# A two-layer pooling and latent-attention trunk on one Trainium2 core: earlier split of the latent key weights, down product's banks handed over one by one, a taller meta matrix

## What is computed

```python
for i in range(DEPTH):                      # DEPTH = 2
    # layer 0: trailing means over windows 2, 4, 8, 16, then a 256x256 product per group
    # layer 1: latent attention: c_q = rms(h @ w_dq), kv = h @ w_dkv (320 wide), 8 heads
    hp = layer_norm(ALPHA * hp + mix_p, ln_g[i, 0], ln_b[i, 0])
    hp = layer_norm(ALPHA * hp + swiglu(hp, ffn_w_gate[i], ffn_w_up[i], ffn_w_down[i]), ln_g[i, 1], ln_b[i, 1])

def swiglu(h, w_gate, w_up, w_down):        # 1024 -> 2816 -> 1024
    return (jax.nn.silu(h @ w_gate) * (h @ w_up)) @ w_down
```

## Time and profile before

| what | value |
|---|---|
| median of 3 runs | 2686.84 us (2685.57 to 2687.7) |
| the profiled execution | 2684.7 us, its span 2682.9 us |
| mean granted TensorE clock | 0.974 |
| TensorE matmuls busy | 2553.1 us (95%), 13203 matmuls |
| VectorE busy | 1005.3 us (37%) |
| ScalarE busy | 567.6 us (21%) |
| GpSimd busy | 585.6 us (22%) |
| DMA | 117.37 MB, 44 GB/s on average |
| both FFNs' gate and up matmuls | 6336, by the three lines 557 to 559 |

### The profile page before, as it was taken

The page is one execution under the profiler, slowest core; times in us unless marked ns, Lnnn a source line. Parts: engine busy times, 40 slices in busy tenths (PEclk is TensorE's granted clock), DMA queues, the critical chain, the costliest instruction groups (busy, mean ns, idle before and its releaser), DMA issues.

```text
span 2682.9 us, 34788 instructions
## 1 busy us (share of the span) xinstructions
PE 2553.1 (95%) x13203; PEld 2122.1 (79%) x13203; DVE 1005.3 (37%) x1489; ACT 567.6 (21%) x948; POOL 585.6 (22%) x290
## 2 busy tenths in 40 slices
PE   8899999999999889899999999988999999999996
PEld 7789888898889776585857584447889988899885
DVE  3433333333333642333333333422333333333336
ACT  2411011110111342332323232433111111111112
POOL 2422222222222410000000000232222222222225
PEclk9999999999999989999999999988999999999998
DMA  5201110111101111000000002232101111011111
GB/s 165 55 24 47 47 47 23 47 47 47 47 23 47 44 48 43 16 1 31 0 19 12 16 0 75 80 122 55 46 25 47 47 47 40 30 47 47 47 31 67
DMA packets 130114, 117.37 MB, mean 44 GB/s; under 512 B 8704, under 2 KB 117208, under 8 KB 130048
## 3 DMA queue, kind: packets, MB, share of 16 engines
q1 hardware_dynamic: 130064, 116.70, 14.6%
HBM read 110.81 MB, written 6.42 MB: 44 GB/s over the span
## 4 chain that ended last, share of the span: by engine, by line
PE 92%; DVE 4%; issue 2%; ACT 1%; POOL 0%; DMA 0%; SPq 0%; ACTq 0%; DVEq 0%
PE ps L557 22%; PE ps L558 21%; PE ps L559 21%; PE ps L922 4%; PE ps L911 4%; PE ps L806 2%; PE ps L895 2%; PE ps L978 1%; PE ps L780 1%; PE ps L822 1%; PE ps L811 1%; PE ps L627 1%; PE ps L953 1%; PE ps L851 1%; PE ps L937 1%
## 5 line engine op out<-in xcount | busy, mean ns | idle before, releaser
L557 PE MATMUL ps<-XH,WGH 128*128 128x368 f32 x2112 | 699.8, 331 | 17.6 <-POOL WGL L1700 13.5
L558 PE MATMUL ps<-XL,WGH 128*128 128x368 f32 x2112 | 700.0, 331 | 0.0
L559 PE MATMUL ps<-XH,WGL 128*128 128x368 f32 x2112 | 697.2, 330 | 0.0
L1452 DVE TENSOR_TENSOR XR<-XR,ps 128x1024 f32<-128x1024 f32 x378 | 461.5, 1221 | 105.7 <-PE ps L559 105.7
L557 PEld LDWEIGHTS ps<-XH,WGH 128*128 128x128 f32 x2112 | 398.5, 189 | 22.3 <-issue 18.9
L1437 DVE TENSOR_TENSOR HF<-SG,ps 128x368 f32<-128x368 f32 x132 | 71.0, 538 | 917.8 <-PE ps L559 912.6
L558 PEld LDWEIGHTS ps<-XL,WGH 128*128 128x128 f32 x2112 | 398.0, 188 | 1.8
L559 PEld LDWEIGHTS ps<-XH,WGL 128*128 128x128 f32 x2112 | 398.2, 189 | 0.0
L557 PE MATMUL ps<-WDH,HH 128*128 128x512 f32 (+1 forms) x792 | 329.4, 416 | 9.6 <-DVE XR L1452 9.6
L1691 POOL TENSOR_TENSOR HL<-HF,HH 128x368 fp32r<-128x368 f32 x132 | 129.8, 983 | 853.0 <-DVE HH L1441 853.0
L559 PE MATMUL ps<-WDH,HL 128*128 128x512 f32 (+1 forms) x792 | 314.9, 398 | 0.0
(11 more groups left out here) (205 smaller groups left out, 2725.8 us busy)
## 6 DMA issues: line engine op xcount, KB each, us to landing
RAWG<-ffn_w_gate SPq DMA_DIRECT2D x44, 512.0 KB, 4.7
RAWG<-ffn_w_up SPq DMA_DIRECT2D x44, 512.0 KB, 5.9
RAWD<-ffn_w_down SPq DMA_DIRECT2D x44, 512.0 KB, 3.7
CR<-cache_mla_l SPq DMA_DIRECT2D x64, 160.0 KB, 2.6
XR<-x_prompt SPq DMA_DIRECT2D x8, 512.0 KB, 12.4
WOP<-mla_w_o SPq DMA_DIRECT2D x4, 1024.0 KB, 5.0
WOA<-mla_w_o SPq DMA_DIRECT2D x1, 4096.0 KB, 17.3
o_y_prompt<-XR SPq DMA_DIRECT2D x8, 512.0 KB, 2.6
```

The costliest lines, as they stand in the source:

```text
L557: pe.matmul(out, w[0], x[0], start=start, stop=False)
L558: pe.matmul(out, w[0], x[1], start=False, stop=False)
L559: return pe.matmul(out, w[1], x[0], start=False, stop=stop)
L1452: dve.tensor_tensor(XR[0:r, t, :], XR[0:r, t, :], bank2(4 + 2 * w, r), ALU.add).then_inc(s_row[2 * l + 1], 1)
```

## The change

There are three parts, and line numbers of the new kernel are about 10 higher.

1. **Down product.** TensorE waits for each bank by itself and signals each half; VectorE adds each half of 512 columns in an instruction of its own. `s_row` and `f_dmm` now count halves, and `s_row` starts at 4 (BANKS). Waits elsewhere are rewritten to the new counts.
2. **Latent key weights.** They get a place of their own, WKRAW, which is the place of WKL: the low part is made in place. SP loads all of them in one DMA after the second chunk's loads; ScalarE copies them after the first chunk's work, VectorE subtracts after it. RAWG then takes the two query halves alone. On SP the loop over chunks starts at 2 instead of 1, the body for 1 being written out.
3. **Meta matrix.** BM gets 80 rows with zeros behind the first 16, and the matmul takes all 80 rows of tile 8.

```diff
-LATENT_HIGH = (0, 3, 7, 10)
-LATENT_LOW = (1, 4, 8, 11)
+LATENT_HIGH = (7, 10)
+LATENT_LOW = (8, 11)
...
+BANKS = 4
...
+        WKRAW = place("WKRAW", [P, DC, ROW], F32, FFN_END + DC * ROW * 4)
...
-            sp.dma_start(BM[0:META], a["c_band_meta"]).then_inc(s_band, 16)
+            sp.dma_start(BM[0:TAIL], a["c_band_meta"]).then_inc(s_band, 16)
...
-                with sp.Fori(1, NF) as n:
+                sp.wait_ge(f_glo[l], 1)
+                load_gate_up(l, 1)
+                sp.wait_ge(f_dlo[l], 1)
+                load_down(l, 1)
+                if l == 0:
+                    sp.wait_ge(s_pool, NT)
+                    sp.wait_ge(s_cast, 3)
+                    sp.dma_start(WKRAW[:], a["mla_w_dkv"][0].rearrange("(c p) n -> p c n", p=P)).then_inc(m_wl, 16)
+                with sp.Fori(2, NF) as n:
...
-            for j, (w, width) in enumerate(LATENT_W):
+            for j in (0, 1):
                 if j == 0:
                     sp.wait_ge(f_glo[0], NF)
                 else:
-                    sp.wait_ge(m_wlo, j)
+                    sp.wait_ge(m_wlo, 2)
...
-                        ins = pe.matmul(o, XR[0:META, 8, ch], BM[0:META, g, :], start=False, stop=True)
+                        ins = pe.matmul(o, XR[0:TAIL, 8, ch], BM[0:TAIL, g, :], start=False, stop=True)
...
-                pe.wait_ge(s_row[2 * l + 1], NT * n + t + 1)
                 for half in (0, 1):
                     ds = slice(half * 512, half * 512 + 512)
-                    ins = split_product(ps[0:r, 4 + 2 * w + half, :], (HH[:, b, cols(t)], HL[:, b, cols(t)]),
-                                        (WDH[:, ds], WDL[:, ds]), True, True)
-                ins.then_inc(f_dmm[l], 1)
+                    pe.wait_ge(s_row[2 * l + 1], 2 * NT * n + 2 * t + half + 1)
+                    split_product(ps[0:r, 4 + 2 * w + half, :], (HH[:, b, cols(t)], HL[:, b, cols(t)]),
+                                  (WDH[:, ds], WDL[:, ds]), True, True).then_inc(f_dmm[l], 1)
...
                     split_down(l, 0)
+                    act.wait_ge(m_wl, 16)
+                    copy(WKH[:], WKRAW[:]).then_inc(m_whi, 1)
...
-                dve.sem_inc(s_row[2 * l + 1], 2)
+                dve.sem_inc(s_row[2 * l + 1], BANKS)
...
-                dve.wait_ge(f_dmm[l], 1 + NT * n + t + 1)
-                dve.wait_ge(s_row[2 * l + 1], NT * n + t + 1)
-                dve.tensor_tensor(XR[0:r, t, :], XR[0:r, t, :], bank2(4 + 2 * w, r), ALU.add
-                                  ).then_inc(s_row[2 * l + 1], 1)
+                for half in (0, 1):
+                    ds = slice(half * 512, half * 512 + 512)
+                    dve.wait_ge(f_dmm[l], 1 + 2 * NT * n + 2 * t + half + 1)
+                    dve.wait_ge(s_row[2 * l + 1], 2 * NT * n + 2 * t + half + 1)
+                    dve.tensor_tensor(XR[0:r, t, ds], XR[0:r, t, ds], ps[0:r, 4 + 2 * w + half, :], ALU.add
+                                      ).then_inc(s_row[2 * l + 1], 1)
...
                 hidden(l, 0, True)
+                if l == 0:
+                    dve.wait_ge(m_whi, 1)
+                    dve.tensor_tensor(WKL[:], WKRAW[:], WKH[:].bitcast(F32), ALU.subtract).then_inc(m_wlo, 1)
...
-    cur, prev, meta = [np.zeros((n, NG, P), f) for n in (P, P, META)]
+    cur, prev, meta = [np.zeros((n, NG, P), f) for n in (P, P, TAIL)]
```

More of the change, by code:

```diff
@@ L473, in _ @@
                 else:
-                    sp.wait_ge(m_wlo, j)
-                dst = RAWG[:].rearrange("p a b c -> p (a b c)")[:, 0:4 * width].rearrange("p (c n) -> p c n", c=4)
-                src = a[w][0].rearrange("(c p) n -> p c n", p=P)[:, 4 * (j % 2):4 * (j % 2) + 4, :]
+                    sp.wait_ge(m_wlo, 2)
+                dst = RAWG[:].rearrange("p a b c -> p (a b c)").rearrange("p (c n) -> p c n", c=4)
+                src = a["mla_w_dq"][0].rearrange("(c p) n -> p c n", p=P)[:, 4 * j:4 * j + 4, :]
                 sp.dma_start(dst, src).then_inc(m_wl, 16)
-            sp.wait_ge(m_wlo, len(LATENT_W))
+            sp.wait_ge(m_wlo, 3)
             for c in range(QC):
                 sp.dma_start(WQPE[:, c], a["mla_w_uq"][0, c * P:(c + 1) * P, :, NOPE:NOPE + ROPE]).then_inc(q_w, 16)
-            sp.wait_ge(f_dmm[0], 1 + NT * (NF - 1))
+            sp.wait_ge(f_dmm[0], 1 + 2 * NT * (NF - 1))
             sp.dma_start(GKV[:], a["mla_g_kv"][0].partition_broadcast(P)).then_inc(m_g, 16)
@@ L572, in ln_transposes @@
                 if k == 1 and t >= 6:
-                    pe.wait_ge(s_row[1], 2 + NT * (NF - 1))
+                    pe.wait_ge(s_row[1], BANKS + 2 * NT * (NF - 1))
                 for c in range(DC):
@@ L677, in last_down @@
                                             (wh[:, ds], wl[:, ds]), b == 0, b == 1)
-                ins.then_inc(f_dmm[l], 1)
+                    ins.then_inc(f_dmm[l], 1)
             def swiglu(l):
@@ L723, in latent_keys @@
                 if t == 0:
-                    pe.wait_ge(m_wlo, 2)
+                    pe.wait_ge(m_wlo, 1)
                     pe.wait_ge(s_xl, NT + 6)
@@ L735, in latent_queries @@
                 if t == 0:
-                    pe.wait_ge(m_wlo, 4)
+                    pe.wait_ge(m_wlo, 3)
                 if t >= 2:
@@ L1062, in split_down @@
                 act.wait_ge(f_rawd[l], 16 * (n + 1))
-                act.wait_ge(f_dmm[l], 1 + NT * n)
+                act.wait_ge(f_dmm[l], 1 + 2 * NT * n)
                 act.wait_ge(f_dlo[l], n)
@@ L1087, in latent_high @@
             def latent_high(j):
-                act.wait_ge(m_wl, 16 * (j + 1))
-                if j == 2:
+                act.wait_ge(m_wl, 16 * (j + 2))
+                if j == 0:
                     act.wait_ge(f_umm[0], 3 * NF)
-                width = LATENT_W[j][1]
-                dst = (WKH if j < 2 else WQH)[:, 4 * (j % 2):4 * (j % 2) + 4, :]
-                copy(dst, RAWG[:].rearrange("p a b c -> p (a b c)")[:, 0:4 * width].rearrange("p (c n) -> p c n", c=4)
-                     ).then_inc(m_whi, 1)
+                copy(WQH[:, 4 * j:4 * j + 4, :], RAWG[:].rearrange("p a b c -> p (a b c)").rearrange(
+                    "p (c n) -> p c n", c=4)).then_inc(m_whi, 1)
             def silu_unit(l, n, even, j):
@@ L1419, in latent_low @@
             def latent_low(j):
-                dve.wait_ge(m_whi, j + 1)
-                part = slice(4 * (j % 2), 4 * (j % 2) + 4)
-                hi, lo = (WKH, WKL) if j < 2 else (WQH, WQL)
-                dve.tensor_tensor(lo[:, part, :],
-                                  RAWG[:].rearrange("p a b c -> p (a b c)")[:, 0:4 * LATENT_W[j][1]].rearrange(
-                                      "p (c n) -> p c n", c=4),
-                                  hi[:, part, :].bitcast(F32), ALU.subtract).then_inc(m_wlo, 1)
+                dve.wait_ge(m_whi, j + 2)
+                part = slice(4 * j, 4 * j + 4)
+                dve.tensor_tensor(WQL[:, part, :],
+                                  RAWG[:].rearrange("p a b c -> p (a b c)").rearrange("p (c n) -> p c n", c=4),
+                                  WQH[:, part, :].bitcast(F32), ALU.subtract).then_inc(m_wlo, 1)
             def hidden_unit(l, n, even, j):
@@ L1439, in hidden_unit @@
                 if j == 0 and not (isinstance(n, int) and n < 1):
-                    dve.wait_ge(f_dmm[l], 1 + NT * (n - 1))
+                    dve.wait_ge(f_dmm[l], 1 + 2 * NT * (n - 1))
                 dve.tensor_copy(HH[:, b, j * TW:(j + 1) * TW], HF[:, q, :]).then_inc(f_hh[l], 1)
@@ L1469, in swiglu @@
                         hidden_unit(l, NF - 1, False, 2)
-                    ln_step(2 * l + 1, t, lambda u: dve.wait_ge(s_row[2 * l + 1], 2 + NT * (NF - 2) + u + 1),
+                    ln_step(2 * l + 1, t, lambda u: dve.wait_ge(s_row[2 * l + 1], BANKS + 2 * NT * (NF - 2) + 2 * u + 2),
                             lambda u: down_add(l, NF - 2, True, u))
@@ L1758, in shape_constants @@
         prev[:, g] = (j - (i - P) < w) / f(w)
-        meta[:, g] = (j - (i[:META] - META) < w) / f(w)
+        meta[:META, g] = (j - (i[:META] - META) < w) / f(w)
         for t in range(META):
```

1 line of the change is left out of this document (removed).

## The result

| | before | changed kernel |
|---|---|---|
| median of the runs taken side by side | 2686.2 us (4 runs, 2684.24 to 2687.7) | 2639.84 us (4 runs, 2636.94 to 2642.02) |
| the profiled execution | 2684.7 us | 2642.02 us |
| its span | 2682.9 us | 2640.2 us |
| mean granted TensorE clock | 0.974 | 0.976 |

The ratio is 0.9827, 95% interval 0.981 to 0.9844: 1.7% faster. The forecast was 2647.6 us with a range from 2643.5. Between the two profiled executions the gain is 42.7 us.

What follows compares the result with a forecast made beforehand. TensorE, 92% of the span, was taken as the bound. Terms -28.0 - 0.2 - 3.55 - 7.5 = -39.25 us gave 2645.5 from the profiled execution, 2647.6 against the median; range 2643.5 to 2658.

Steps and rivals of the forecast that it cites:

- A: Start: TensorE's clock rises only 17.5 us after the start, so the meta matrix brings -2.3; 2652.8 us in all; 20%.
- B: Down phases: VectorE keeps up only nearly, 0.76 us per half's add, holding 0.2 us a phase; 2656 us; 5%.
- C: Down phases: the hold is not the bank and stays, only parts 2 and 3 count; 2676 us; 3%.
- D: Down phases: VectorE becomes the pace, its adds blocked by GpSimd's 4.66 us subtraction; slower, 2800 us; 3%.
- E: FFN loops: without holds the granted clock falls to 0.97 in both 720 us stretches; +43, 2691 us; 2%.
- 40 x 0.70: Down product in the loops: 0.70 us of hold vanishes in each of 40 phases; -28.0 us.
- pace limit of 0.745: Down phase: VectorE's adds in a row hold nothing up to 0.745 us per half.
- Per FFN -0.1: FFN ends, half adds: tile 2 gains 0.53 us, six later tiles pay 0.07 each; together -0.2 us.
- one such meeting may come or go: First FFN's end, latent key weights: VectorE's SBUF work stretches beside GpSimd, giving bounds -1.5 and -5 us.
- -3.55: First FFN's end, latent key weights: VectorE's second subtraction of 3.62 us goes, and all that follows moves along; -3.55 us.
- -7.5: Start, 80-row meta matrix: tile 0 runs at full pace, first x16 group ends at 22.1 against 29.6; -7.5 us.
- The rule of few operations: FFN ends: VectorE's pipe is flushed after each operation, six tiles pay 0.19 each; sum 1.4 us higher, about 2649.

Runs made afterwards that it cites:

- experiment 8: Against the changed kernel: VectorE makes each half's add as four adds of 128 columns; 2664.94 us, ratio 0.9927.
- experiment 1: Against the kernel before: only the bank-by-bank down product, without latent key weights or meta matrix changes; 2650.53 us, ratio 0.9872.
- experiment 5: Against the changed kernel: TensorE waits for both banks of a tile at once, VectorE still adds in halves; 2639.03 us, ratio 0.9837.
- experiment 7: Against the changed kernel: VectorE makes each half's add as two adds of 256 columns; 2635.78 us, ratio 0.9827.
- experiment 9: Against the changed kernel: GpSimd zeros the meta matrix, only 16 rows loaded; second FFN's end, VectorE takes gain and bias of tiles 5, 7, 8; 2636.49 us.
- experiment 11: Against the changed kernel: ScalarE's first-chunk copy of the key weights made four times in a row; 2639.24 us, ratio 0.9834.

## Why the prediction was right, and where it was wrong

**The sign and the mechanism of each of the three parts** came out as argued. No rival happened: the clock rose early (A), VectorE kept pace (B), the hold was the bank (C), no add was blocked (D), the clock in the loop stayed at 1.00 (E).

**Part 1, the term 40 x 0.70.** Mis-sized: 0.747 was measured, 1.9 us in all (another 0.2 of the loops' 30.1 lies outside the down phases). The step "13.23 us against 54 x 0.232 = 12.53" used one phase and a rounded turn; 54 free products take 12.50 (0.2315 each), and the mean phase before was 13.24. Five hundredths of a microsecond count when they stand forty times. The pace limit of 0.745 was right to 0.01 (experiment 8), the price of an add, 0.69, too.

**Part 1, the term "Per FFN -0.1" at the FFNs' ends.** This step failed, and the lower bound of the range let it move by nothing. It counted VectorE's instructions and took their distance for given; measured in experiment 1 are -2.2 (with the latent products behind) and -2.3. The second end is 74.6 us in each of the three profiles without part 1, and 72.2 to 72.8 in the eight with halves of 512 columns and the same `LN_VECTOR` there. At that end the reason is a meeting with GpSimd. Here are VectorE's bias of tile 5 and GpSimd's next gain, before and after, from the timelines of both engines:

```profile
2665.15 3.40 DVE L1364 TENSOR_TENSOR XR<-XR,GB 128x1024 f32<-128x1024 f32 x1
```

```profile
2665.12 2.34 POOL L1682 TENSOR_TENSOR XR<-XR,GB 128x1024 f32<-128x1024 f32 x1 [1.09 <-ACT XR L379]
```

```profile
2624.36 1.22 DVE L1373 TENSOR_TENSOR XR<-XR,GB 128x1024 f32<-128x1024 f32 x1
```

```profile
2624.44 3.34 POOL L1694 TENSOR_TENSOR XR<-XR,GB 128x1024 f32<-128x1024 f32 x1 [1.21 <-ACT XR L381]
```

Before, GpSimd began 0.03 us ahead, and VectorE's 1.22 us became 3.40. After, VectorE began 0.08 us ahead and took 1.22; GpSimd's 2.4 became 3.34. A shift of a tenth of a microsecond is worth 2.2 us on VectorE, which sets this end. The Trainium skill, "SBUF — State Buffer", section "SBUF: two separate sides", says that one of the two engines takes a shared port pair for its whole instruction and the other is blocked; by that rule the VectorE row should end 1.2 us after GpSimd's 2667.46, and it ends 1.1 us after it, at 2668.55. The forecast quoted this stretching for part 2 ("one such meeting may come or go", -1.5 to -5) and left it out for part 1, where it came.

At the first end the adds bring 0.2 us in experiment 1, and 2.0 come behind it: TensorE is back at full clock 3.4 us after resuming instead of 5.8, and a little more at the later gaps of the same stage. Why, and how much of it is part 1's, stays open. The latent products take 141.8 to 142.1 us in the three profiles without part 1; with it they take 139.4 to 140.6 in eight and 142.0 in three (experiments 5, 7 and 8). A meeting plays in here too. In the changed kernel and in experiment 5, VectorE's bias of tile 2:

```profile
896.01 3.46 DVE L1373 TENSOR_TENSOR XR<-XR,GB 128x1024 f32<-128x1024 f32 x1
```

```profile
895.50 1.22 DVE L1373 TENSOR_TENSOR XR<-XR,GB 128x1024 f32<-128x1024 f32 x1
```

GpSimd began 0.02 us ahead of the first (895.99) and 0.02 us behind the second (895.52); the end took 75.3 and 73.0 us. Experiment 5 lost the difference again in latent products at half clock. Experiments 9 and 11, whose code is the same there, did not: 73.0 + 139.4 = 212.4 and 73.0 + 140.6 = 213.6, against 215.1. So this stretch alone moves by 2.7 us.

**Part 2.** -3.55 was forecast at the end of the first FFN, and -3.6 measured in the kernel that has this part alone; 0 in the first chunk was right. The load took 6.9 us, not 9, so the cover was 3.1 us and not 0.9.

**Part 3.** -7.5 forecast, -7.3 and -7.1 in the two profiles of the changed kernel. Here luck helped, as two errors cancelled: the start came at 9.43 and not at 8.2, and the pace doubled after 4.5 us and not after 6. The 0.35 us that the forecast charged to the 128 KB are not shown: experiment 1 loads 16 rows and started at 9.45.

**The rule of few operations** (the Trainium skill, "VectorE: DVE Perf Modes", section "Rules for kernel authors") would have put the sum 1.4 us higher. The rows speak against it: behind another an add of 512 columns costs 0.59, one of 128 only 0.198, and the ends became shorter, not longer.

**The number and the range.** Profile to profile, the terms fell short by 3.4 us: 2.1 in the loops, 4.5 at the ends, 0.2 before, less 3.4 that the sample stage took back. The other 4.3 us between the forecast of 2647.6 and the median come from the level. The forecast added 2.1 us, the distance from the profile of before to its median, where the changed kernel's profiled execution lay 2.2 us above its own median. The range had no term for a stage that alone moved from 157.5 to 167.7 us over the profiles (below), and none for the ends of the FFNs. A spread of 3 us to either side for it, and -5 at the ends as for part 2, would have held the result.

## What to carry to other kernels

When TensorE alternates between few banks, cut the instruction that frees them into pieces of one bank: a producer that is held 0.7 us in each phase then runs free, until the pieces of a bank take longer together than the products that fill it. Price short instructions by the distance of their starts in a row, not by their records, and read who waits from the waiting engine's row. Where two engines block each other, don't forecast such a stretch to better than the length of one blocked instruction, and take the bound from both orders.
